# Where the tiles of a two-layer hybrid decoder lie in SBUF: the arena directly behind the normalised input

## What is computed

```python
for l in range(DEPTH):
    mod = (c_act @ ada_w[l] + ada_b[l]).reshape(bsz, N_SUBLAYERS, 3, D_MODEL)
    h = _modulate(_rmsnorm(x, ffn1_norm[l]), mod[:, 0, 0], mod[:, 0, 1])
    x = x + 0.5 * (1.0 + mod[:, 0, 2])[:, None, :] * _swiglu(h, ffn1_w1[l], ffn1_w3[l], ffn1_w2[l])
    h = _modulate(_rmsnorm(x, mix_norm[l]), mod[:, 1, 0], mod[:, 1, 1])
    y = _hybrid_mixer(h, ...)
    x = x + (1.0 + mod[:, 1, 2])[:, None, :] * y
    h = _modulate(_rmsnorm(x, ffn2_norm[l]), mod[:, 2, 0], mod[:, 2, 1])
    x = x + 0.5 * (1.0 + mod[:, 2, 2])[:, None, :] * _swiglu(h, ffn2_w1[l], ffn2_w3[l], ffn2_w2[l])
```

## The kernel before

| tile | address before | address after |
|---|---|---|
| x | 16,512 | 160,000 |
| h_hi, h_lo | 32,896 and 49,280 | 16,512 and 32,896 |
| raw (2 tiles of 4 KB) | 65,664 | 176,384 |
| w_hi, w_lo (4 tiles of 4 KB each) | 73,856 and 90,240, up to 106,624 | 184,576 and 200,960, up to 217,344 |
| c_act, vectors and constants; nones_r, ntri_r | 106,624 to 116,704; 113,888, 114,400 | 217,344 to 227,424; 224,608, 225,120 |
| arena | 116,704 | 49,280 |
| g_hi, g_lo | 116,704 and 161,760 | 49,280 and 94,336 |
| ya_hi, ya_lo | 116,704 and 133,088 | 49,280 and 65,664 |
| yf_hi, yf_lo | 116,704 and 124,896 | 49,280 and 57,472 |
| ys_hi, ys_lo | 149,472 and 157,664 | 82,048 and 90,240 |
| mx_hi, mx_lo | 182,240 and 198,624 | 114,816 and 131,200 |
| wab_hi, xa_hi (first of two) | 190,432 and 194,528 | 123,008 and 127,104 |
| v_hi, e_hi (first of two) | 190,432 and 203,744 | 123,008 and 136,320 |

## Time and profile before

### The profile page before, as it was taken

How to read it: one execution, slowest core, us unless ns; L and a number is a source line. 1 busy time by engine, 2 the same in 40 slices (tenths; PEclk the granted TensorE clock), 3 DMA queues, 4 the chain that set the end, 5 groups by cost and what they waited for, 6 DMA issues and landing times.

```text
span 2788.3 us, 31913 instructions
## 1 busy us (share of the span) xinstructions
PE 2688.9 (96%) x13172; PEld 2250.3 (81%) x13172; DVE 1285.1 (46%) x1612; ACT 1058.8 (38%) x1592; POOL 1161.6 (42%) x468
## 2 busy tenths in 40 slices
PE   3999999999999999999999999999999999999998
PEld 3888888878878888888888888887888788888887
DVE  6666337866442133511056663477545412453111
ACT  5222236644443234222252222565443332522223
POOL 2555444532223434545435554354222243354542
PEclk9999999999999999999999999999999999999999
DMA  5655532221112223422245554222111122253322
GB/s 220 211 184 202 176 122 103 85 74 53 61 53 76 92 92 129 174 98 99 95 140 197 195 192 166 96 91 91 53 61 61 46 98 91 78 186 131 98 99 76
DMA packets 90833, 323.82 MB, mean 116 GB/s; under 512 B 10048, under 2 KB 12480, under 8 KB 90432
## 3 DMA queue, kind: packets, MB, share of 16 engines
q1 hardware_dynamic: 90688, 321.78, 34.0%
HBM read 319.64 MB, written 2.10 MB: 115 GB/s over the span
## 4 chain that ended last, share of the span: by engine, by line
PE 85%; DVE 8%; ACT 4%; issue 1%; POOL 1%; DMA 1%; SPq 0%; ACTq 0%; DVEq 0%
PE bank L1222 26%; PE bank L1220 26%; PE bank L1221 26%; PE bank L1255 2%; PE bank L1371 1%; PE bank L1260 1%; DVE e_lo L1046 1%; DVE e_f L1074 1%; DVE e_hi L1044 1%; PE bank L1404 1%; DVE e_f L1039 1%; POOL w_lo L417 1%; DVE ada L1120 1%; DVE gt L946 1%; ACT w_hi L447 1%
## 5 line engine op out<-in xcount | busy, mean ns | idle before, releaser
L417 POOL TENSOR_TENSOR w_lo<-raw,w_hi 128x1024 fp32r<-128x1024 f32 x440 | 1141.3, 2604 | 1513.9 <-ACT w_hi L447 1513.6
L1220 PE MATMUL bank<-h_hi,w_hi 128*128 128x512 f32 x2240 | 877.0, 392 | 9.7 <-POOL w_lo L417 9.5
L1221 PE MATMUL bank<-h_lo,w_hi 128*128 128x512 f32 x2240 | 874.1, 390 | 0.0
L1222 PE MATMUL bank<-h_hi,w_lo 128*128 128x512 f32 x2240 | 873.7, 390 | 0.0
L447 ACT ACTIVATE w_hi<-raw 128x1024 fp32r<-128x1024 f32 x440 | 463.7, 1056 | 975.7 <-PE bank L1222 895.7
L1220 PEld LDWEIGHTS bank<-h_hi,w_hi 128*128 128x128 f32 x2240 | 421.9, 188 | 98.6 <-issue 10.2
L1222 PEld LDWEIGHTS bank<-h_hi,w_lo 128*128 128x128 f32 x2240 | 421.4, 188 | 89.0
L1221 PEld LDWEIGHTS bank<-h_lo,w_hi 128*128 128x128 f32 x2240 | 421.8, 188 | 87.5
L790 DVE CUSTOM_DVE_ANT_0 ada<-ada,c_act 128x1024 f32<-128x1024 f32 x144 | 287.7, 2006 | 234.0 <-DMA ada<-ada_w 234.0
L1222 PE MATMUL bank<-g_hi,w_lo 128*128 128x512 f32 (+1 forms) x792 | 295.2, 373 | 0.0
L1221 PE MATMUL bank<-g_lo,w_hi 128*128 128x512 f32 (+1 forms) x792 | 292.3, 369 | 0.0
(11 more groups left out here) (210 smaller groups left out, 3073.8 us busy)
## 6 DMA issues: line engine op xcount, KB each, us to landing
raw<-w_units SPq DMA_DIRECT2D x440, 512.0 KB, 3.5
ada<-ada_w SPq DMA_DIRECT2D x144, 512.0 KB, 4.9
ada<-ada_w SPq DMA_DIRECT2D x8, 1024.0 KB, 16.6
x<-x_in SPq DMA_DIRECT2D x4, 512.0 KB, 6.9
wab_raw<-wab SPq DMA_DIRECT2D x2, 1024.0 KB, 5.9
y<-fin SPq DMA_DIRECT2D x8, 256.0 KB, 2.1
c_act<-c_rows SPq DMA_DIRECT2D x1, 512.0 KB, 3.8
vec<-vecs SPq DMA_DIRECT2D x3, 92.5 KB, 3.5
```

The lines of the kernel that those rows point to most:

```text
L417: nc.gpsimd.tensor_tensor(w_lo[s][:, :, :], raw[u % RAW][:, :, :], w_hi[s][:, :, :].bitcast(F32), ALU.subtract).then_inc(unit_lo.sem, 1)
L1220: nc.tensor.matmul(o, wh, xh, start=start, stop=False, skip_group_check=True)
L1221: nc.tensor.matmul(o, wh, xl, start=False, stop=False, skip_group_check=True)
L1222: return nc.tensor.matmul(o, wl, xh, start=False, stop=stop, skip_group_check=True)
```

## The change

`x` is no longer the first tile. `h_hi` and `h_lo` are, and the arena follows directly behind them; `x`, `raw`, `w_hi`, `w_lo`, the vectors and the constants follow above the arena in their old order. No instruction, semaphore, transfer, shape or order of work differs, only the address of each tile (the table above).

```diff
-        x = sb("x", [P, KD, T])
         h_hi = sb("h_hi", [P, KD, T], F32R)
         h_lo = sb("h_lo", [P, KD, T], F32R)
+
+
+        base = (nc.sbuf_base + 31) // 32 * 32
+        ARENA = 110720
+        sb("arena", [P, ARENA // 4])
+
+        x = sb("x", [P, KD, T])
         raw = [sb(f"raw{i}", [P, UB, P]) for i in range(RAW)]
         w_hi = [sb(f"w_hi{i}", [P, UB, P], F32R) for i in range(RING)]
         w_lo = [sb(f"w_lo{i}", [P, UB, P], F32R) for i in range(RING)]
@@ -162,10 +168,6 @@
         wf_hi = sb("wf_hi", [P, KD, HEADS], F32R)
         wf_lo = sb("wf_lo", [P, KD, HEADS], F32R)
 
-
-        base = (nc.sbuf_base + 31) // 32 * 32
-        ARENA = 110720
-        sb("arena", [P, ARENA // 4])
```

## The result

The change made the kernel slower. The median went from 2790.97 us (2790.31 to 2791.97, four runs) to 2821.61 us (2819.72 to 2824.14, four runs), a ratio of 1.0110 with a 95% interval of 1.0093 to 1.0128. The forecast was 2772.5 us. The profiled execution of the changed kernel has a span of 2818.7 us against 2788.3, 30.4 us more, at the same granted clock of 0.992. Its lines are numbered two higher: L1222 to L1224 here are L1220 to L1222 of before.

A forecast was written before the change was run, and what follows sets the result against it. The prediction took the pace of TensorE's matmuls to bound the kernel. Gains of 12.3 + 1.9 + 2.6 + 1.6 + 0.5 = 18.9 us off 2790.0 gave 2771.1, plus 1.3 for the median: 2772.5 us, range 2768 to 2795.

The forecast's parts named there:

- What bounds the kernel: TensorE, busy for 96% of the span and 85% of the last chain: only the pace of the matmuls changes the time.
- Which property of the place: Alignment to a 64-byte line, rather than region or height, makes h (226.6 ns a matmul) faster than g (233.3); 56%.
- The sum of step (1): Arena matmuls against w take h's pace: g 12.3 us, mx 1.9, ys and yf 2.6, ya 1.6, settling 0.5; 18.9 us.
- Step (2): x, raw and the constants move up: taken as 0, with 2 us kept either way.
- a sign that I named there: Groups of ScalarE, VectorE or GpSimd (L447, L417, L858) changing by more than 2% would show the forecast wrong in another way.
- Step (3): A faster down phase asks for weight units every 5.44 us instead of 5.60; nothing new ends late.
- The slower rival: h by w loses its pace and goes to 233.3 ns: 6430 matmuls, 43 us, 2834 us; 22% with its unsettled variant.
- its sign, `h_lo` in 690 to 700: In the slower rival, `h_lo` steps in 690 to 700 ns for a triple; the forecast had it stay at 680.
- The unsettled variant: Within the slower rival: h only fails to settle, runs at 230 ns and costs 22 us, arena gains 9: 2804 us.
- The rule about the ports: TensorE's read ports for moving operand and weight loads are independent, so placement would do nothing; named as speaking against the forecast.

## Why the prediction was wrong

**What bounds the kernel** held: nothing but the pace of the matmuls moved the time, by 18 us down or 30 up.

**Which property of the place: here it failed.** The step read out of rows 3, 4, 6 and 7 that a pair is fast when moving and stationary tile stand alike to a 64-byte line. By that, distance 128 is as good as 0, and so the sum has no term for h at all: h was to keep its 226.6 ns. It went to 232.4 ns, and its 512-column matmuls took 35.9 us more. That moving and stationary tile count together was right (the run with everything moved by 96 bytes); the unit was wrong, 256 bytes instead of 64 (the runs at 64, 128 and 192). The trace of before had only two distances: 0 (h by w, xa by wab, e by v, e by `ntri_r`) and 96 (the arena by w). With one fast and one slow class, every period that puts 96 apart from 0 fits, 64, 128 or 256. They part only at the place where the change put h, distance 128, and no row covered that.

The single matmuls of rows 6 and 7 were also weaker than they looked. The 96 matmuls of xa by wab have a median step of 231 ns in before and 227 with the arena at distance 0, though their own distance is 0 in both. A short run among others doesn't show its own pace, and a least value out of few shows it even less.

**The sum of step (1)** was right as a price of something else. Putting the arena at distance 0 gave 18.3 us of span where the sum said 18.9, and 3.0 us in a down phase where it said 3.1 (12.3 / 4). Step by step g gained 12.4 us (12.3 forecast), mx 1.9 (1.9), ys and yf 2.8 (2.6) and ya 2.2 (1.6).

**Step (2)**, no price for the place of x, raw and the constants, held: the changed kernel and the one with its distances in the regions of before have spans of 2818.7 and 2818.6. But a sign that I named there misled: a group of VectorE that changes by over 2%. L858 went from 1935 to 1989 ns (2.8%), and in the kernel with only the arena padded it is at 2006, with a gain of 17 us. It moves with the timing: of its 88 instructions those that start outside a GpSimd instruction of L417 take 0.68 us, all others 1.4 to 2.9, and 83 start inside one before, 86 after and 86 in that kernel.

**Step (3)**, nothing new ends late, held but for one place: the wait for `xa_lo`, 4.7 us in one execution at the fast pace and 0.4 in another.

**The slower rival** (22%) named the mechanism, "128 bytes matter as 32 do", and its sign, `h_lo` in 690 to 700, is what came. Its price was too high, 43 us (2834) where 30.4 came. Its terms: h by w cost 35.9 us and not 43, because 6.7 ns became 5.8 (226.6 to 232.4) and because in the mixers h, which was not at its full pace there before either, paid 10.6 us on 960 triples, where 17.4 ns each would be 16.7. And what isn't h by w at 512 columns gained 5.5 us, where the rival let the arena stay as it was. The unsettled variant (2804) was too low.

**The rule about the ports.** The runs show 680 against 687 to 703 ns for a triple by nothing but padding, and the run with w_lo alone at 128 points to the load of the next weights as one of the parties. The Trainium skill, "SBUF — State Buffer", section "Who interferes with whom", calls TensorE's two read ports independent. By that no padding would have moved the time; the measurement decides against it for this pair of streams. The other engines ran in all of these kernels, so the runs don't exclude that one of them has a part. The steps speak against it: in 300:390 of before those of g are 230 to 231, 230 to 231 and 238 to 239 ns in every triple, while the other engines start and stop beside them.

## What to carry to other kernels

Where fp32r matmuls of 512 columns with a fresh weight tile each bound a kernel, write down the address of the moving tile less that of the weights, modulo 256 bytes, for each family, and try padding until it is 0: here 160 bytes were worth 0.6% and 128 bytes in the wrong place cost 1.2%. Other shapes and formats were not tried; the 256-column matmuls of this kernel gained nothing from distance 0. Any change of the allocation, even one that adds no instruction, can shift all of these at once, so the distances belong beside the allocation as an assertion. And when a trace has one fast and one slow class, a reading that fits both is not yet a rule for a third place: ask first whether the change lands on a point that the trace contains.

## What the runs showed of the hardware

| distance mod 256 | ns for a triple (family) |
|---|---|
| 0 | 680 (h; arena) |
| 32 | 700 (h) |
| 64 | 687 (arena; h from the second up phase on), 700 (h in the first) |
| 96 | 700 (arena) |
| 128 | 697 or 700, by stretch (h, arena) |
| 160 | 703 (arena) |
| 192 | 700 (arena) |
| 224 | 700 (h) |

All paces at full clock are 680 ns plus a multiple of 6.7 ns, or nearly so, shared out over the train: 687, 693 and 700 are one, two and three such delays in three matmuls, 697 would be six in seven (680 + 3 x 6/7 x 6.67 = 697.1) and 703 eight in seven (702.9). 6.67 ns would be 16 cycles at 2.4 GHz, and 226.67 ns 544 of them, the granted clock being 1.00 in these stretches of before. That is a reading of the numbers; what in the chip waits 16 cycles was not shown. At the lower clock, 1.2 GHz, the step is 426.7 ns, 512 cycles, at distance 0 and 128 alike: both the delays and the 32 cycles above 512 are gone. A tile out of place makes a matmul late whose own distances to the weights are all 0 (by a delay carried over, or by the distance of one moving tile to the next, which wasn't tested), and with the same tiles the train can stay for a whole phase in one of two patterns. At distance 0 the FFN stretches of all kernels showed only one.

A second surprise lies on VectorE, off the path. The 144 instructions that form the modulation vector, by group, before and after:

```profile
L790 DVE CUSTOM_DVE_ANT_0 ada<-ada,c_act 128x1024 f32<-128x1024 f32 x144 | 287.7, 2006 | 234.0 <-DMA ada<-ada_w 234.0
```

```profile
L792 DVE CUSTOM_DVE_ANT_0 ada<-ada,c_act 128x1024 f32<-128x1024 f32 x144 | 250.5, 1747 | 283.4 <-DMA ada<-ada_w 283.0
```

13% less, all of it given back as idle time before their transfers. With the regions of before and the distances of after the mean is 1783 ns, with all at distance 0 it is 1968. The trace tells why. The instructions that start while GpSimd is within a `w_lo<-raw,w_hi` (L417) take 1.5 to 3.5 us, mean 3.0; all others take 1.21 to 1.23. Before, 63 of the 144 start so, after 42. So with the slower rhythm fewer of them start behind a GpSimd instruction, and the addresses need no part in it. No run moved one engine's work against the other's to confirm it.
